# Feed-forward up slots in pairs by seven block products in place of eight, with weight block sums and gate times up on GpSimd

## The chip, the cores and the metric

The kernel runs on one core of one Trainium2 chip. The metric is device time in microseconds (us) of one execution. All data are f32. Every product is made in three fp32r passes: weights and activations are split into a high and a low part, and high x high, high x low and low x high are added in PSUM.

## What is computed

A two-layer block and then a second block, over 512 tokens of width 1024. Only the first block's feed-forward parts (two in each layer, four in all) are touched:

```python
def swiglu(x, w_gu, w_down):
    g, u = jnp.split(x @ w_gu, 2, axis=-1)
    return (jax.nn.silu(g) * u) @ w_down
...
h = h + 0.5 * swiglu(rmsnorm(h, ffn1_norm[i]), ffn1_w_gu[i], ffn1_w_down[i])
...
h = h + 0.5 * swiglu(rmsnorm(h, ffn2_norm[i]), ffn2_w_gu[i], ffn2_w_down[i])
```

The inner width is 2816, which is 22 tiles of 128 rows; each tile has a gate half and an up half. Between the two feed-forward parts of a layer stand a convolution branch and an attention branch, after them a gated projection; the second block follows the two layers. None of that is changed.

## The kernel before

**Slots.** The program is a list of slots. A slot is one weight tile of up to 8 x 128 rows by 128 columns: SyncE loads it into one of four places of `raw` (`load`), ScalarE copies it as fp32r into `w_hi` (`split_hi`, L673), VectorE writes `raw - w_hi` into `w_lo` (`split_lo`, L1688), and TensorE multiplies it with the 512 tokens in one of the four PSUM banks of `proj` (`slot_mm`, L1194 to L1196: for each of 8 k tiles three matmuls of 512 columns, 24 in all). Each engine has its own program in order; counters (`slot_done`, `slot_read`, `w_hi_ready`, `w_lo_ready`) hold them together. VectorE and ScalarE split a slot two slots before TensorE takes it (`AHEAD`).

**A feed-forward part** (`ffn` on each engine) has three groups of 8, 8 and 6 tiles (`FF_GROUPS`). A group is an up stage (two slots a tile, gate then up) and a down stage (8 slots that add to `h`). Behind each pair of up slots VectorE scales both results by `rs`, the inverse norm (L1704, from PSUM), ScalarE takes the tanh (L720), VectorE makes (tanh + 1) x gate (L1769) and times up (L1773), ScalarE rounds that to `a_hi` (L724), and VectorE takes the rest as `a_lo` (L1776). GpSimd does nothing in the up stages. It works in the last down stage of each part, where it squares and adds the columns of the new `h` for the next norm (`squares`, L563 to L568).

**The start of a part.** TensorE begins with slot 0 as soon as the normalized input `u_hi`, `u_lo` arrives, then makes the norm sum (L1215); ScalarE takes a root, VectorE the reciprocal `rs` (L1698), and only then are the results of the first slots read. The four banks hold them until then.

Of the kernel before, what the change touches and what calls it, by code (L numbers as in the profile page):

```python
# [147 lines left out]
def build(nc, I, out_t):  # L148
    ctx = ExitStack()
    with ctx:  # L150
# [25 lines left out]
        w_lo, _ = place("w_lo", RING * KD * P, F32R)  # L176
# [101 lines left out]
        pos_ready, sin_ready, c_tanh, lam_exp = (sem(n) for n in ("pos_ready", "sin_ready", "c_tanh", "lam_exp"))  # L278
# [20 lines left out]
        out_done = sem("out_done")  # L299

# [20 lines left out]


# [83 lines left out]
        HALF = S // 2  # L406
# [17 lines left out]
        def _(sp):  # L424
# [53 lines left out]
            for layer in range(DEPTH):  # L478
# [54 lines left out]
        def _(pool):  # L533
# [2071 lines left out]
```

## Time and profile before

| | us |
|---|---|
| median of 3 runs | 3029.08 (3026.34 to 3031.82) |
| the profiled execution, its own time | 3027.1 |
| its span in the trace | 3025.4 |
| VectorE busy | 1691.3 (56%) |
| ScalarE busy | 1104.4 (37%) |
| GpSimd busy | 303.9 (10%) |

The span runs from the first to the last instruction in the trace. A busy share is an average over stages, and says little of a single one. The prediction reads a stage from its own rows. A matmul's recorded duration has its way through the array in it, so that its pace is read from the distance between the starts of two matmuls, not from the duration.

### The profile page before, as it was taken

The page shows a single profiled execution, that of the slowest core. Times are in us where ns is not written, and L with a number is a line of the kernel's source. Part 1 is how long each engine was busy: PE and PEld are TensorE (multiplying, and loading weights), DVE is VectorE, ACT ScalarE, POOL GpSimd, SP SyncE. Part 2 cuts the span into 40 slices and gives each one's busy share as a digit, 9 for nine tenths or more (in the row PEclk, how much of TensorE's full clock was granted, in tenths as well). Part 3 has the DMA queues.
Part 4 walks back from the last instruction along what each step waited for, and adds up shares of the span by engine and source line. Part 5 has one row for each costly group of instructions (what it writes and reads, how often), then busy time and mean ns, then how long its engine had stood idle before and what let it go on. Part 6 is the DMA issues. An engine that isn't in the chain of part 4 may idle for free.

```text
span 3025.4 us, 36951 instructions
## 1 busy us (share of the span) xinstructions
PE 2989.9 (99%) x13582; PEld 2432.9 (80%) x13582; DVE 1691.3 (56%) x2381; ACT 1104.4 (37%) x1717; POOL 303.9 (10%) x248
## 2 busy tenths in 40 slices
PE   8999999999999999999999999999999999999999
PEld 7888888778888887888888888888888775688887
DVE  6655564565655557555456455555556767463334
ACT  4232333562332234322232454232323555552223
POOL 2000300000100012000030000200003215600000
PEclk9999999999999999999999999999999998999999
DMA  5332232123323223432232212333222420122232
GB/s 199 109 125 95 94 98 78 58 60 115 139 97 139 97 87 95 152 139 97 92 97 96 84 38 78 111 139 141 96 97 84 170 70 29 43 79 96 95 94 82
DMA packets 86804, 301.55 MB, mean 100 GB/s; under 512 B 10272, under 2 KB 19616, under 8 KB 85536
## 3 DMA queue, kind: packets, MB, share of 16 engines
q1 hardware_dynamic: 86688, 300.02, 30.0%
q8 instruction: 71, 1.16, 0.2%
q14 instruction: 45, 0.37, 0.0%
HBM read 297.88 MB, written 2.10 MB: 99 GB/s over the span
## 4 chain that ended last, share of the span: by engine, by line
PE 93%; DVE 3%; ACT 2%; POOL 1%; issue 1%; DMA 0%; DVEq 0%; SPq 0%; ACTq 0%
PE proj L1194 27%; PE proj L1196 27%; PE proj L1195 27%; PE ot L1341 1%; PE proj L1575 1%; PE proj L1577 1%; PE proj L1576 1%; DVE w_lo L1688 1%; PE sc L1575 1%; PE sc L1577 1%; PE sc L1576 1%; POOL work L644 1%; PE ot L1468 0%; PE tr L1301 0%; PE sc L1290 0%
## 5 line engine op out<-in xcount | busy, mean ns | idle before, releaser
L1194 PE MATMUL proj<-u_hi,w_hi 128*128 128x512 f32 x2632 | 1029.5, 391 | 13.6 <-DVE u_lo L1693 9.0
L1196 PE MATMUL proj<-u_hi,w_lo 128*128 128x512 f32 x2632 | 1021.6, 388 | 0.0
L1195 PE MATMUL proj<-u_lo,w_hi 128*128 128x512 f32 x2632 | 1021.6, 388 | 0.0
L1688 DVE TENSOR_TENSOR w_lo<-raw,w_hi 128x1024 fp32r<-128x1024 f32 (+4 forms) x567 | 657.2, 1162 | 492.1 <-ACT w_hi L673 482.9
L673 ACT ACTIVATE w_hi<-raw 128x1024 fp32r<-128x1024 f32 (+4 forms) x567 | 535.9, 954 | 334.9 <-PE proj L1196 212.9
L1194 PEld LDWEIGHTS proj<-u_hi,w_hi 128*128 128x128 f32 x2632 | 494.8, 188 | 122.8 <-issue 15.9
L1195 PEld LDWEIGHTS proj<-u_lo,w_hi 128*128 128x128 f32 x2632 | 495.0, 188 | 104.1 <-issue 3.1
L1196 PEld LDWEIGHTS proj<-u_hi,w_lo 128*128 128x128 f32 x2632 | 494.7, 188 | 101.9
L1194 PE MATMUL proj<-a_hi,w_hi 128*128 128x512 f32 x936 | 368.1, 393 | 3.4 <-DVE w_lo L1688 1.5
L1196 PE MATMUL proj<-a_hi,w_lo 128*128 128x512 f32 x936 | 364.9, 390 | 0.0
L1195 PE MATMUL proj<-a_lo,w_hi 128*128 128x512 f32 x936 | 364.5, 389 | 0.0
L1704 DVE TENSOR_TENSOR work<-proj,rs 128x512 f32<-128x512 f32 x260 | 179.3, 690 | 279.7 <-PE proj L1196 279.2
L724 ACT ACTIVATE a_hi<-work 128x512 f32 (+1 forms) x88 | 55.6, 632 | 437.3 <-DVE work L1773 437.3
L1194 PEld LDWEIGHTS proj<-a_hi,w_hi 128*128 128x128 f32 x936 | 175.8, 188 | 42.2 <-DVE a_lo L1776 3.0
L1196 PEld LDWEIGHTS proj<-a_hi,w_lo 128*128 128x128 f32 x936 | 175.7, 188 | 37.1
L1195 PEld LDWEIGHTS proj<-a_lo,w_hi 128*128 128x128 f32 x936 | 175.9, 188 | 34.7
L563 POOL TENSOR_TENSOR acc<-h 128x512 f32<-128x512 f32 x6 | 6.2, 1040 | 1500.7 <-DVE h L1791 1301.6
L1791 DVE SCALAR_TENSOR_TENSOR h<-proj,h 128x512 f32<-128x512 f32 x96 | 66.3, 691 | 159.6 <-PE proj L1196 159.5
L720 ACT ACTIVATE work<-work 128x512 f32<-128x512 f32 x88 | 55.6, 632 | 261.3 <-DVE work L1704 261.3
L1776 DVE TENSOR_TENSOR a_lo<-work,a_hi 128x512 f32 (+1 forms) x88 | 61.0, 693 | 78.9 <-ACT a_hi L724 78.9
L679 ACT ACTIVATE u_hi<-h,vec 128x512 fp32r<-128x512 f32 x48 | 34.8, 725 | 141.0 <-DVE h L1791 82.1
L566 POOL TENSOR_TENSOR sq<-h 128x512 f32<-128x512 f32 x42 | 62.1, 1479 | 72.4 <-DVE h L2041 40.0
(469 smaller groups left out, 2879.7 us busy)
## 6 DMA issues: line engine op xcount, KB each, us to landing
raw<-in_ffn_gu SPq DMA_DIRECT2D x174, 512.0 KB, 3.4
raw<-in_in_w SPq DMA_DIRECT2D x68, 512.0 KB, 3.3
raw<-in_ffn_dn SPq DMA_DIRECT2D x64, 512.0 KB, 3.3
raw<-in_ff SPq DMA_DIRECT2D x64, 512.0 KB, 3.4
gate<-in_ada SPq DMA_DIRECT2D x8, 3072.0 KB, 12.0
raw<-in_ffn_dn SPq DMA_DIRECT2D x32, 384.0 KB, 3.0
raw<-in_in SPq DMA_DIRECT2D x18, 512.0 KB, 3.4
raw<-in_mla_out SPq DMA_DIRECT2D x16, 512.0 KB, 3.4
```

Of the source, the lines that this page charges most:

```text
L566: pool.tensor_tensor(sq, x(m), x(m), ALU.mult).then_inc(sq_ready, 1)
L673: act.activation(wt(w_hi, slot, slot.tiles), wt(raw, slot, slot.tiles), ACT.Copy)\
L1194: pe.matmul(out, w_h, x_h, start=first, stop=False)
L1195: pe.matmul(out, w_h, x_l, start=False, stop=False)
L1196: return pe.matmul(out, w_l, x_h, start=False, stop=last)
L1575: pe.matmul(row_bank(half, t), span(hi(k), t), w_h, start=first and j + i == 0, stop=False, skip_group_check=True)
L1576: pe.matmul(row_bank(half, t), span(lo(k), t), w_h, start=False, stop=False, skip_group_check=True)
L1577: mm = pe.matmul(row_bank(half, t), span(hi(k), t), w_l, start=False, stop=last and j + i == 2, skip_group_check=True)
L1688: dve.tensor_tensor(wt(w_lo, slot, slot.tiles), wt(raw, slot, slot.tiles), wt(w_hi, slot, slot.tiles).bitcast(F32), ALU.subtract).then_inc ...
L1704: return dve.tensor_tensor(dst, proj[:, slot.pos, :], rs, ALU.mult)
L1776: dve.tensor_tensor(a_lo_t[:, at], work(8 + q), a_hi_t[:, at].bitcast(F32), ALU.subtract)\
L1791: dve.scalar_tensor_tensor(at, proj[:, slot.pos, :], 0.25, at, ALU.mult, ALU.add)\
```

## The change

In 72 of the 88 pairs of up slots (the first round of four slots of each part, and in the very first part the whole first group, stay as they are) the product of a pair of weight tiles with the tokens is made from blocks. The 1024 input rows are cut into two halves, the two tiles (gate and up) are the two block columns, and the 512 tokens are cut into two halves of 256. A 2 x 2 block product needs eight block products; Strassen's scheme, in Winograd's form, needs seven with sums of blocks. A block product is here 4 k tiles x 3 passes = 12 matmuls of 256 columns.

- TensorE (`pair_products`): 7 x 12 = 84 matmuls of 256 columns for each pair, in place of 48 of 512. A pair uses four half banks; three of them are used twice. Even pairs use `proj`, odd pairs `tr`, `ot` and `sc`.
- GpSimd (`pair_sums`): four weight block sums of 512 columns for each pair, written to `w_sum`, which lies on `w_lo`. It also adds the parts of the results (two adds of 256 columns, `part_sum`) and multiplies gate and up (`gate_times_up`, 512 columns).
- ScalarE: splits 3.5 x 1024 columns of weights for a pair (`pair_hi`) where it was 2 x 1024, and copies four parts of 256 columns from PSUM (`part_copy`); tanh and `a_hi` as before.
- VectorE: subtracts for 3.5 x 1024 columns (`pair_lo`), adds parts from PSUM (`first_half` 256 columns, `other_halves` 512), scales gate and up by `rs` in one instruction of 1024 columns in SBUF, then `pair_act` (tanh + 1 times gate x up) and `pair_a_lo` of 512 each.
- A weight place is now shared: a pair's block i lies where the pair before had its block i, and may be written once that product is done (`place_free`).
- At the start of each part, in the round of ordinary slots, sums of blocks of the input are made (`x_diffs`, 4 blocks): on VectorE five instructions of 1024 columns and later four of 1024 or 2 x 512 for the low parts, on GpSimd six of 512 and two of 1024, on ScalarE four splits.
- The first two down slots of each group are interleaved over k up to the last k tile. SyncE's load of the gated projection's input (`p_t`) is issued after the second part's last weights rather than before them. Several counters of other stages share one counter.

Cut to its core, the diff is:

```diff
-w_lo, _ = place("w_lo", RING * KD * P, F32R)
+w_lo, w_lo_at = place("w_lo", RING * KD * P, F32R)
+w_sum, _ = place("w_sum", RING * KD * P, at=w_lo_at)
...
+def paired_rounds(no, g):
+    return 0 if g < start_group(no) else FF_GROUPS[g] // 2 - (g == start_group(no))
...
+def done(self, i):
+    return ((slot_done, self.up.done) if self.odd and i == 6 else
+            (product_done, 13 * self.round + 7 * self.odd + i + 1))
+def place_free(self, i):
+    if self.opening or (i == 6 and not self.odd):
+        return slot_done, self.start.number + 1 + i // 2
+    return (product_done, 13 * self.round + i + 1) if self.odd else (product_done, 13 * (self.round - 1) + 7 + i + 1)
+def place(self, t, i, n=1):
+    o = (2 * self.start.pos + i) % (2 * RING) * S
...
+def banks(self):
+    if self.odd:
+        return tr[:, 0:HALF], ot[:, 0:HALF], sc[:, 0:2, 0:HALF]
+    p = self.start.pos
+    p2 = (p + 2) % RING
+    return proj[:, p, 0:HALF], proj[:, p + 1, 0:HALF], proj[:, p2:p2 + 2, 0:HALF]
...
+def pair_sums(p, which):
+    a11, a12 = (wt(raw, p.gate, KD)[:, j * S:(j + 1) * S] for j in range(2))
+    a21, a22 = (wt(raw, p.up, KD)[:, j * S:(j + 1) * S] for j in range(2))
+    s1, s3, s2, s4 = (p.place(w_sum, i) for i in (2, 3, 4, 5))
+    if which == 0:
+        pool.wait_ge(raw_in[p.gate.pos], p.gate.loads)
+        pool.wait_ge(raw_in[p.up.pos], p.up.loads)
+        pool.wait_ge(*p.place_free(2))
+        pool.tensor_tensor(s1, a21, a22, ALU.add).then_inc(block_sum, 1)
+        pool.wait_ge(*p.place_free(3))
+        pool.tensor_tensor(s3, a11, a21, ALU.subtract).then_inc(block_sum, 1)
+        return
+    pool.wait_ge(*p.place_free(4))
+    pool.wait_ge(block_sum, 4 * p.number + 1)
+    pool.tensor_tensor(s2, s1, a11, ALU.subtract).then_inc(block_sum, 1)
+    pool.wait_ge(*p.place_free(5))
+    pool.wait_ge(block_sum, 4 * p.number + 3)
+    pool.tensor_tensor(s4, a12, s2, ALU.subtract).then_inc(block_sum, 1)
...
+spare = t4_raw[:, 0:S]
+for j in range(2):
+    k = slice(2 * j, 2 * j + 2)
+    to = t3_raw(j)
+    step(four(to), x_hi_lo(u_hi_t, 1, 1)[:, k].bitcast(F32), x_hi_lo(u_hi_t, 0, 1)[:, k].bitcast(F32), ALU.subtract)
+    step(four(spare), x_hi_lo(u_lo_t, 1, 1)[:, k].bitcast(F32), x_hi_lo(u_lo_t, 0, 1)[:, k].bitcast(F32), ALU.subtract)
+    step(to, to, spare, ALU.add)
+pool.wait_ge(x_diff, XD * no + 5)
+step(four(t4_raw), x_hi_lo(u_hi_t, 1, 0).bitcast(F32), four(d_at(xd_f, 3)), ALU.subtract)
+step(four(t4_raw), four(t4_raw), x_hi_lo(u_lo_t, 1, 0).bitcast(F32), ALU.add)
...
+def gate_times_up(p):
+    pool.wait_ge(pair_scaled, p.number + 1)
+    pool.tensor_tensor(p.both[:, S:2 * S], p.both[:, 0:S], p.both[:, S:2 * S], ALU.mult).then_inc(sil_ready, 1)
+def ffn(layer, f):
+    no = 2 * layer + f
+    for g in range(start_group(no), len(FF_GROUPS)):
+        pairs = pairs_of(layer, f, g)
+        if g == start_group(no):
+            x_diffs(layer, f)
+        pair_sums(pairs[0], 0)
+        pair_sums(pairs[0], 1)
+        for n, p in enumerate(pairs):
+            after = pairs[n + 1:n + 2]
+            if n:
+                gate_times_up(pairs[n - 1])
+            for q in after:
+                pair_sums(q, 0)
+            pool.wait_ge(part_copied, p.copied + 3)
+            pool.tensor_tensor(part_b, part_b, part_c, ALU.add).then_inc(part_sum, 1)
+            for q in after:
+                pair_sums(q, 1)
+            pool.wait_ge(part_copied, p.copied + 4)
+            pool.wait_ge(part_sum, 2 * p.number + 1)
+            pool.tensor_tensor(p.both[:, 3 * HALF:4 * HALF], part_b, part_d, ALU.add).then_inc(part_sum, 1)
+        gate_times_up(pairs[-1])
...
+def part_copy(p, i):
+    product, bank, to = ((0, p.banks()[0], part_a), (2, p.banks()[2][:, 0], part_b),
+                         (3, p.banks()[2][:, 1], part_c), (4, p.banks()[0], part_d))[i]
+    act.wait_ge(*p.done(product))
+    if i == 0:
+        act.wait_ge(slot_read, p.start.number + RING + 2 * p.odd)
+    if i == 1 and p.number:
+        act.wait_ge(part_sum, 2 * p.number)
+    act.activation(to, bank, ACT.Copy).then_inc(part_copied, 1)
...
+for n, p in enumerate(pairs):
+    after = pairs[n + 1] if n + 1 < len(pairs) else None
+    pair_hi(p, 3)
+    part_copy(p, 0)
+    if n:
+        pair_tanh(pairs[n - 1])
+    if after:
+        pair_hi(after, 0)
+    else:
+        split_hi(down[0])
+    part_copy(p, 1)
+    part_copy(p, 2)
+    if n:
+        pair_a_hi(pairs[n - 1])
+    elif a_hi_before:
+        a_hi_before()
+        act.wait_ge(x_diff_pool, XP * no + 8)
+        act.wait_ge(slot_done, p.start.number + RING)
+        act.activation(x_hi_lo(u_hi_t, 0, 1), four(t4_raw), ACT.Copy).then_inc(x_diff_hi, 1)
+    part_copy(p, 3)
+    if after:
+        pair_hi(after, 1)
+        pair_hi(after, 2)
+    else:
+        split_hi(down[1])
...
+for i, (bank, n_half, opens) in enumerate(((b0, 0, True), (b1, 0, True), (b2, 0, True), (b3, 0, True),
+                                           (b0, 0, False), (b2, 1, False), (b3, 1, False))):
+    if i in (0, 1, 5, 6):
+        k_half = (0, 1, 0, 0, 0, 1, 0)[i]
+        x_h, x_l = (part(t, k_half, n_half) for t in (u_hi_t, u_lo_t))
+    else:
+        x_h, x_l = diff((0, 0, 0, 2, 1)[i])
+    if i == 2:
+        pe.wait_ge(block_lo, 2 * p.number + 2)
+        pe.wait_ge(x_diff, XD * p.no + 8)
+        if not p.odd:
+            pe.wait_ge(slot_read, p.start.number + RING)
+    if i == 4:
+        pe.wait_ge(w_lo_ready, p.gate.done)
+        pe.wait_ge(part_copied, p.copied + 1)
+    if i == 5:
+        pe.wait_ge(part_copied, p.copied + 2)
+    if i == 6:
+        pe.wait_ge(w_lo_ready, p.up.done)
+        pe.wait_ge(part_copied, p.copied + 3)
+        pe.wait_ge(x_diff, XD * p.no + 9)
+    for k in range(KD // 2):
+        w_h, w_l = p.weight(i, k)
+        mm = pe.matmul(bank, w_h, x_h(k), start=opens and k == 0, stop=False, skip_group_check=True)
+        if p.odd and k == 0 and i in (2, 4, 6):
+            mm.then_inc(slot_done, 1)
+        pe.matmul(bank, w_h, x_l(k), start=False, stop=False, skip_group_check=True)
+        mm = pe.matmul(bank, w_l, x_h(k), start=False, stop=k == KD // 2 - 1, skip_group_check=True)
+    mm.then_inc(slot_done if p.odd and i == 6 else product_done, 1)
...
+def first_half(p):
+    dve.wait_ge(*p.done(1))
+    dve.wait_ge(part_copied, p.copied + 1)
+    dve.tensor_tensor(p.both[:, 0:HALF], p.banks()[1], part_a, ALU.add).then_inc(slot_read, 1)
+def other_halves(p):
+    b23 = p.banks()[2]
+    dve.wait_ge(*p.done(6))
+    dve.wait_ge(part_copied, p.copied + 4)
+    dve.tensor_tensor(four(p.both[:, HALF:3 * HALF]), b23, part_d.unsqueeze(1).to_broadcast([P, 2, HALF]), ALU.add)\
+       .then_inc(slot_read, 1)
+    dve.wait_ge(*p.scaled())
+    dve.wait_ge(part_sum, 2 * p.number + 2)
+    both = p.both.rearrange("p (n s) -> p n s", n=2)
+    dve.tensor_tensor(both, both, rs.unsqueeze(1).to_broadcast([P, 2, S]), ALU.mult).then_inc(pair_scaled, 1)
+def pair_act(p):
+    dve.wait_ge(tanh_ready, p.count)
+    dve.wait_ge(sil_ready, p.count)
+    up = p.both[:, S:2 * S]
+    dve.scalar_tensor_tensor(up, work(4 + p.odd), 1.0, up, ALU.add, ALU.mult).then_inc(act_ready, 1)
...
+for n, p in enumerate(pairs):
+    after = pairs[n + 1] if n + 1 < len(pairs) else None
+    if n:
+        other_halves(pairs[n - 1])
+    pair_lo(p, 2)
+    pair_lo(p, 3)
+    if n == 0 and before:
+        before[0]()
+    first_half(p)
+    if after:
+        pair_lo(after, 0)
+    else:
+        split_lo(down[0])
+    if n:
+        pair_act(pairs[n - 1])
+        pair_a_lo(pairs[n - 1])
+    elif before:
+        before[1]()
+        dve.wait_ge(x_diff_hi, XH * no + 4)
+        dve.tensor_tensor(x_hi_lo(u_lo_t, 0, 1), four(t4_raw), x_hi_lo(u_hi_t, 0, 1).bitcast(F32), ALU.subtract)\
+           .then_inc(x_diff, 1)
+    if after:
+        pair_lo(after, 1)
+    else:
+        split_lo(down[1])
+other_halves(pairs[-1])
+pair_act(pairs[-1])
+pair_a_lo(pairs[-1])
```

## Rows read from the trace of the kernel before

**Rows 1.** The page: busy time by engine, and the chain that ended last.
```profile
PE 2989.9 (99%) x13582; PEld 2432.9 (80%) x13582; DVE 1691.3 (56%) x2381; ACT 1104.4 (37%) x1717; POOL 303.9 (10%) x248
PE 93%; DVE 3%; ACT 2%; POOL 1%; issue 1%; DMA 0%; DVEq 0%; SPq 0%; ACTq 0%
```
**Rows 2.** Waits of TensorE: waiting line, releaser, total us, times, longest.
```profile
PE proj L1194 <- DVE u_lo L1693: 9.0, 2, 8.4
PE proj L1194 <- DVE w_lo L1688: 3.1, 5, 0.8
```
**Rows 3.** Timeline of TensorE, 512 columns: start us, us; 30 matmuls lie between them.
```profile
2373.78 0.39 PE L1194 MATMUL proj<-u_hi,w_hi 128*128 128x512 f32 x1
...
2380.58 0.39 PE L1194 MATMUL proj<-u_hi,w_hi 128*128 128x512 f32 x1
```
**Rows 4.** Timeline of TensorE, 256 columns, second block: 30 matmuls from first to last.
```profile
2678.53 0.28 PE L1194 MATMUL proj<-u_hi,w_hi 128*128 128x256 f32 x1
...
2682.12 0.28 PE L1194 MATMUL proj<-u_hi,w_hi 128*128 128x256 f32 x1
```
**Rows 5.** Groups by form, stretch 810 to 850 us: count, busy us, mean ns, idle before.
```profile
L1688 DVE TENSOR_TENSOR w_lo<-raw,w_hi 128x1024 fp32r<-128x1024 f32 x8 | 9.8, 1226 | 10.0 <-ACT w_hi L673 9.7
L673 ACT ACTIVATE w_hi<-raw 128x1024 fp32r<-128x1024 f32 x7 | 7.3, 1046 | 0.0
L1704 DVE TENSOR_TENSOR work<-proj,rs 128x512 f32<-128x512 f32 x8 | 5.5, 690 | 5.8 <-PE proj L1196 5.8
L1773 DVE TENSOR_TENSOR work<-work 128x512 f32<-128x512 f32 x4 | 2.8, 692 | 0.4
L720 ACT ACTIVATE work<-work 128x512 f32<-128x512 f32 x4 | 2.5, 633 | 8.5 <-DVE work L1704 8.5
```
**Rows 6.** Groups by form, GpSimd, whole span.
```profile
L588 POOL TENSOR_TENSOR work<-work 128x512 f32<-128x512 f32 x6 | 7.8, 1293 | 44.0 <-ACT work L822 44.0
L578 POOL TENSOR_TENSOR acc<-acc,work 128x512 f32<-128x512 f32 x6 | 11.1, 1856 | 0.9
L644 POOL TENSOR_SCALAR work<-work,row_stats 128x512 f32<-128x512 f32 x16 | 24.9, 1571 | 13.6 <-DVE row_stats L2136 13.6
L644 POOL TENSOR_SCALAR work<-work,row_stats 128x256 f32<-128x256 f32 x8 | 7.3, 920 | 3.9 <-DVE row_stats L2136 3.9
```
**Rows 7.** Timeline of GpSimd and VectorE near 750 us: GpSimd began first.
```profile
750.59 1.28 POOL L568 TENSOR_TENSOR acc<-acc,sq 128x512 f32<-128x512 f32 x1
750.70 2.26 DVE L1688 TENSOR_TENSOR w_lo<-raw,w_hi 128x1024 fp32r<-128x1024 f32 x1 [1.08 <-ACT w_hi L673]
```
**Rows 8.** Timeline of both engines near 350 us: VectorE began first.
```profile
349.87 0.96 DVE L1688 TENSOR_TENSOR w_lo<-raw,w_hi 128x768 fp32r<-128x768 f32 x1 [0.87 <-ACT w_hi L673]
349.98 2.00 POOL L568 TENSOR_TENSOR acc<-acc,sq 128x512 f32<-128x512 f32 x1
```
**Rows 9.** Timeline of both engines near 2374 us: they take turns.
```profile
2373.49 1.29 POOL L613 TENSOR_TENSOR acc<-acc,work 128x512 f32<-128x512 f32 x1 [3.49 <-ACT work L900]
2374.17 1.16 DVE L2058 SCALAR_TENSOR_TENSOR h<-work,h 128x512 f32<-128x512 f32 x1
2374.74 1.74 POOL L614 TENSOR_TENSOR sq<-sq,ax 128x512 f32<-128x512 f32 x1
2375.26 1.51 DVE L1688 TENSOR_TENSOR w_lo<-raw,w_hi 128x256 fp32r<-128x256 f32 x1
```
**Rows 10.** Timeline near 587 us: VectorE reads PSUM and one SBUF tile.
```profile
586.28 1.29 POOL L594 TENSOR_TENSOR ux<-ux,sq 128x512 f32<-128x512 f32 x1 [40.19 <-ACT ux L766]
586.93 0.69 DVE L1921 TENSOR_TENSOR u_lo<-ot,u_hi 128x512 fp32r<-128x512 f32 x1
```
**Rows 11.** Timeline, VectorE at the start of the second feed-forward part.
```profile
787.93 3.35 DVE L1698 RECIPROCAL rs<-acc 128x512 f32<-128x512 f32 x1 [4.22 <-ACT acc L683]
791.20 1.16 DVE L1688 TENSOR_TENSOR w_lo<-raw,w_hi 128x1024 fp32r<-128x1024 f32 x1
```
**Rows 12.** Windows: from:to, us, busy us (x instructions) by engine, PEclk, DMA share, GB/s.
```profile
2388.00:2392.00 4.00, 2.00 (x5) 0.57 (x3) 2.18 (x4) 3.45 (x6) 0.00 (x0) 1.00 0.85 360
2510.00:2515.00 5.00, 2.20 (x15) 1.54 (x13) 4.69 (x11) 0.42 (x1) 0.19 (x1) 0.99 0.27 105
2515.00:2520.00 5.00, 4.73 (x42) 2.80 (x44) 1.76 (x6) 1.52 (x4) 0.00 (x0) 0.50 0.02 5
```

More of the change, by code:

```diff
@@ new lines, in pairs_of @@
+        def pairs_of(layer, f, g):
+            return [Pair(layer, f, g, at) for at in range(2 * paired_rounds(2 * layer + f, g))]
+        HALF = S // 2
+        XD, XP, XH = 9, 8, 4
+        x_at = work_at + 8 * S * 4
+        xd_r, _ = place("x_split", 10 * S, F32R, at=x_at)
+        xd_f, _ = place("x_diffs", 10 * S, at=x_at)
+        four = lambda x: x.rearrange("p (k s) -> p k s", s=HALF)
+        x_hi_lo = lambda x_t, k_half, n_half: x_t.rearrange("p (m s) -> p m s", s=S)[
+            :, KD // 2 * k_half:KD // 2 * (k_half + 1), HALF * n_half:HALF * (n_half + 1)]
@@ L323, in build @@
+        d_at = lambda t, i: t[:, 2 * i * S:2 * (i + 1) * S]
+        t3_lo = lambda j: (a_hi_t, a_lo_t)[j][:, 8 * S:9 * S]
+        t3_raw = lambda j: (ax(8), ax(17))[j]
+        t4_raw = ax_t[:, 6 * S:8 * S]
+        part_a, part_b, part_c, part_d = (work_t[:, 6 * S + j * HALF:6 * S + (j + 1) * HALF] for j in range(4))
         L2 = DEPTH
@@ new lines, in pair_tanh, with pair_a_hi, paired @@
+            def pair_tanh(p):
+                act.wait_ge(pair_scaled, p.number + 1)
+                act.activation(work(4 + p.odd), p.both[:, 0:S], ACT.Tanh, scale=0.5).then_inc(tanh_ready, 1)
+            def pair_a_hi(p):
+                act.wait_ge(act_ready, p.count)
+                act.activation(a_hi(p.tile), p.both[:, S:2 * S], ACT.Copy).then_inc(a_hi_ready, 1)
+            def paired(layer, f, g, a_hi_before):
+                no = 2 * layer + f
+                down = [Slot(layer, STAGE[f"ffn{f + 1}_down{g}"] + j) for j in range(AHEAD)]
+                pairs = pairs_of(layer, f, g)
+                for n, p in enumerate(pairs):
[23 more added lines that the diff above has]
+                        split_hi(down[1])
+                pair_tanh(pairs[-1])
+                pair_a_hi(pairs[-1])
@@ L1775, in up @@
-                            at = bass.ds((2 * it + q) * S, S)
-                            dve.tensor_tensor(a_lo_t[:, at], work(8 + q), a_hi_t[:, at].bitcast(F32), ALU.subtract)\
-                               .then_inc(a_lo_ready, 1)
-                    repeat(dve, s0, ft // 2, RING, up, first or passed)
+                            if starts:
+                                (x_diffs_lo if q else x_diffs)(no)
+                            if starts and q:
+                                pair_lo(Pair(layer, f, g, 0), 1)
+                            elif 2 * q + 1 + AHEAD >= opened:
+                                split_lo(Slot(layer, s0 + 2 * q + 1 + AHEAD, it, RING))
```

325 lines of the change are left out of this document (252 added, 73 removed).

## The prediction

> **What bounds the kernel now.** I read the page first. TensorE is busy for 99% of the span, and 93% of the chain that ended last is TensorE [rows 1]. Its longest waits sum to 12 us, and 8.4 of them are one wait at the very start [rows 2]. So the kernel ends when TensorE has issued its matmuls, and in the stages that are changed nothing else is late: in 40 us of an up stage VectorE waits 15.8 us ahead of its splits and scalings [rows 5]. The timeline then gives the pace. Between the two starts of [rows 3] lie 30 matmuls of 512 columns: 6.80 / 30 = 0.2267 us each. A pair of up slots is 48 of them, 10.88 us. This is the time against which each part below stands.
>
> **What TensorE saves.** Matmuls of 256 columns with their own weights stand in the second block: 3.59 / 30 = 0.1197 us each [rows 4]. The 84 of a pair take 10.05 us, so a pair saves 0.83 us and 72 pairs 59 us. The weight loads do not bind at that pace.
> The Trainium skill, "TensorE: Matmul & The Clock Gate", section "Back-to-back issue gap", gives 131 ns for 512 columns and 81 ns for 128 in a sustained stream, which would be about 98 ns for 256 (an estimate between its two figures). By it a pair would go from 6.3 to 8.2 us and the change would lose 1.9 us a pair. The trace does not agree (227 and 120 ns), and I go by the trace.
>
> **What the helpers must do in a pair.** Taken one by one, each engine fits under 10.05 us. VectorE: `pair_lo` 3 x 1.226 + 0.69, the scaling 1.226, `pair_act` and `pair_a_lo` 2 x 0.692, and from PSUM 0.69 and about 0.4: 8.1 us [rows 5]. ScalarE: 3 x 1.046 + 0.6 for weights, four copies of 256 columns at about 0.4, two of 0.633: 6.6 us [rows 5]. GpSimd: five instructions of 512 columns at 1.293 and two of 256: I take 0.75 for one of these, between half of 1.293 and 0.92, the row of a one-input instruction of that width; 8.0 us in all [rows 6].
>
> **But VectorE and GpSimd do not run side by side.** In [rows 7] GpSimd's add ends at 751.87. VectorE's split, begun 0.11 us after it, takes 2.26 us where 1.226 is usual [rows 5] and ends 1.09 us after GpSimd's end. In [rows 8] it is the other way round: VectorE ends at 350.83, and GpSimd's add takes 2.00 in place of 1.293 and ends 1.15 us after that. In [rows 9] they take turns four times: ends at 2374.78, 2375.33, 2376.48 and 2376.77, so 0.55 us for VectorE with 512 columns, 1.15 for GpSimd, 0.29 for VectorE with 256. Whole instructions exclude each other where VectorE reads two SBUF operands. Where it reads PSUM and one SBUF operand they don't: 0.69 us in the middle of a GpSimd add, as without it [rows 10].
> [...] Were the contention partial, the sum below would shrink towards the fast rival's; the trace shows a full block.
>
> So I add the claims of both engines on this one resource, at 1.09 / 0.55 us for 1024 / 512 columns on VectorE and 1.15 on GpSimd:
> - VectorE: `pair_lo` 0, 1, 2 and the scaling, 4 x 1.09; `pair_lo` 3, `pair_act`, `pair_a_lo`, 3 x 0.55: 6.0 us.
> - GpSimd: four block sums and gate times up, 5 x 1.15; two adds of 256 columns, 0.58 to 0.78 each, taken as 0.6: 6.95 us.
> Together 13.0 us. I followed the two orders in the diff once round. Counted from the end of a pair's scaling: `pair_lo` 2 to 1.1, gate times up 2.3, `pair_lo` 3 2.8, sum 1 4.0, `pair_lo` 0 5.1, sum 3 6.3, `pair_act` 6.8, part add 7.4, sum 2 8.6, `pair_a_lo` 9.1, sum 4 10.3, `pair_lo` 1 11.4, part add 12.0, next scaling 13.2. Each is ready when its turn comes, so the period is 13.2 us. TensorE's products 4, 5, 6, 0 and 1 follow `pair_lo` 2 and end at 8.4; it then waits 3 us for `pair_lo` 1 before product 2. ScalarE has half of its time free. Bounds: 12.6 (the 256-column adds at their least and less for each turn) to 14.2 (1 us a period in which the resource lies idle between a semaphore and the next start).
>
> **The waits that are added.** TensorE's product 2 waits for `pair_lo` 1, and with it all later products; `pair_lo` 1 stands behind `pair_a_lo` and that behind ScalarE's `a_hi`. VectorE's scaling waits for GpSimd's last add, which stands behind block sums 2 and 4 of the next pair; behind the scaling stand the next pair's `pair_lo` 2 and 3, for which products 4 and 6 wait. This ring runs through both engines.
>
> **The sum.**
> 1. Interior pairs. The groups have 6 pairs (eight of them) or 8 (three). First and last pair have less to do: no pair before, no pair after. So 8 x 4 + 3 x 6 = 50 periods of 13.2 in place of 10.88: +116 us (86 to 166).
> 2. Ends of 11 groups. From the first product to the first scaling's end I count 13.4 us, and from the last interior scaling to TensorE's last product 5.5: 18.9 in place of 21.8, so -2.9 each, -32 us. What follows in the down stage is covered: the last `a_lo` is ready 7 us after the last product, and the first two down slots have 42 matmuls (9.5 us) that do not need it.
> 3. Starts of 4 parts. In the four ordinary slots the resource must carry `x_diffs` on VectorE (5 x 1.14 one behind the other), on GpSimd 6 x 1.15 + 2 x 2.3, the low parts 3.4, four block sums 4.6, and the usual splits and products, 6.4: some 32 us. `rs` comes at 791.3, five us after slot 0 is done [rows 11]; behind it VectorE has a split, the first scaling and then the five `x_diffs` before the split of slot 3. That split ends near 803.6 and TensorE wants it at 798.8: 4.8 us. `pair_lo` 0 is late by 4.6, `pair_lo` 1 by 4.0, slot 2 by 0.8, and the first pair's backlog is 4 us longer than in other groups: 18 us, in three of the parts. The first part starts it in its second group, where `rs` is long there: 15. Together +69 us (35 to 100).
> 4. Nothing: the moved load of `p_t` (issued at the start of the last down stage, some 35 us before it is read, and the queue in front of it has then only weights already asked for), the counters shared by stages, ScalarE's work, weight traffic (1 MB a pair in 10 us or more, where windows show up to 360 GB/s [rows 12]), and more program code to fetch. If code does not come in time, some us each group; covered by the range.
>
> 116 - 32 + 69 = +153 us. On the profiled execution's 3027.1 that is 3180; the median of the runs stands 2 us higher, so 3182.
>
> **The rivals.**
> - *TensorE stays the bound (faster).* If the claims of both engines overlap after all, or fall between each other's waits, each engine alone is under 10.05 us and the pairs run at TensorE's pace: -59, and about 3 us at each start: 3027 - 59 + 12 = 2980. The point from which it decides is a joint claim under 10.05 us. For it: busy sums of 8 us. Against it: three stretches with full exclusion [rows 7 to 9]. Chance 0.09.
> - *Slower still by the clock.* TensorE would wait 3 us in each period. After 2.28 us and 0.8 us of waiting in a window with little work its granted clock went to 0.50, the lower level, 1.2 GHz, in the next window; after a wait of 2.0 in 4 us it stayed at 1.00 [rows 12]. If it falls in most periods, the matmuls behind a wait take twice as long for about 5 us. Part of that goes into the wait itself; I take 1.5 us of a period and 6 us of a start: 50 x 1.5 + 4 x 6 = +99, 3281. Chance 0.17.
> - *Same.* If block sums slip into times in which VectorE works from PSUM or waits, and starts cost 8 us, gains and losses could cancel: a period of 11.2: 50 x 0.3 - 32 + 32, about 3042, with zero inside its spread. Chance 0.03.
> The rest, 0.71, is the forecast. What this kernel's measurement can tell from no change is 0.2%, 6 us. Faster 0.09, same 0.03, slower 0.88. The range reaches from the low ends of steps 1 and 3 (3027 + 86 - 32 + 35 = 3116, a little less for a period under 12.6) into the clock case: 3095 to 3275.
>
> **What the profile would show.** GpSimd and VectorE each busy most of the up stages, their instructions stretched: block sums of 512 columns at a mean of 1.7 to 2.3 us, `pair_lo` of 1024 columns near 1.9 to 2.2. Scaling instructions 13.2 us apart within a group. TensorE waiting for `pair_lo` before product 2, some 3 us a pair, its busy share near 93%, and 15 to 20 us lost at each start. Matmuls of 256 columns 0.12 us apart between waits. Wrong if the scalings stand 10.1 us apart and the block sums take 1.3 us: then two SBUF operands do not exclude GpSimd here, and the time is near 2980. The clock case shows as PEclk under 1.0 in the up stages and matmuls 0.24 us apart.

## The result, and the profile of the changed kernel

| | before | after |
|---|---|---|
| median of the runs, us | 3028.97 (3026.34 to 3031.82, 4 runs) | 3198.56 (3197.45 to 3200.09, 4 runs) |
| profiled execution, us | 3027.1 | 3200.1 |
| its span, us | 3025.4 | 3198.4 |

The changed kernel takes 1.056 times as long (95% interval 1.0542 to 1.0578). The forecast was 3182, within 3095 to 3275.

The page after: busy time by engine, and the chain that ended last; they answer to [rows 1].
```profile
PE 3008.8 (94%) x16174; PEld 2566.7 (80%) x16174; DVE 2187.2 (68%) x2565; ACT 1313.5 (41%) x2160; POOL 1189.0 (37%) x784
PE 68%; DVE 17%; POOL 7%; issue 5%; ACT 2%; DMA 0%; SPq 0%; DVEq 0%; POOLq 0%; ACTq 0%
```
TensorE was 93% of the chain and is 68% of it now; VectorE and GpSimd have 24% between them. GpSimd looks idle for 63% of the span. That is an average over stages, and says nothing of the up stages.

The waits of TensorE after (waiting line, releaser, total us, times, longest), against some 12 us in all in [rows 2]:
```profile
PE proj L1544 <- DVE work L2113: 69.7, 24, 3.3
PE sc L1544 <- DVE w_lo L2068: 32.8, 23, 2.7
PE proj L1544 <- DVE w_lo L2068: 20.0, 4, 11.5
PE proj L1448 <- DVE w_lo L2005: 13.8, 10, 3.6
PE proj L1544 <- DVE work L2021: 10.5, 4, 4.2
PE proj L1544 <- DVE u_lo L2154: 9.9, 4, 3.7
```
L1544 is the first matmul of each three in a pair's product, L2068 a 1024-column `pair_lo`, L2113 the addition of `other_halves` that empties the pair's PSUM banks. The first two rows are 47 waits in the middle of groups. The other four belong to the starts of the parts, but for seven waits of under 0.8 us in the fourth row.

Groups by form of the whole span after (count, busy us, mean ns, idle before); they answer to [rows 5, 6]:
```profile
L2068 DVE TENSOR_TENSOR w_lo<-w_sum,w_hi 128x1024 fp32r<-128x1024 f32 x72 | 142.5, 1980 | 40.8 <-POOL w_sum L680 40.8
L2118 DVE TENSOR_TENSOR work<-work,rs 128x1024 f32<-128x1024 f32 x72 | 88.2, 1225 | 18.6 <-POOL work L734 13.5
L676 POOL TENSOR_TENSOR w_sum<-raw 128x512 f32<-128x512 f32 x72 | 151.0, 2098 | 1.9 <-PE proj L1548 1.9
L712 POOL TENSOR_TENSOR work<-work 128x512 f32<-128x512 f32 x72 | 148.7, 2065 | 120.4 <-DVE work L2118 120.4
L683 POOL TENSOR_TENSOR w_sum<-raw,w_sum 128x512 f32<-128x512 f32 x72 | 127.3, 1768 | 10.6 <-POOL w_sum L680 0.4
L674 POOL TENSOR_TENSOR w_sum<-raw 128x512 f32<-128x512 f32 x72 | 122.2, 1697 | 261.8 <-PE proj L1450 191.3 <-PE proj L1548 68.8 <-PE sc L1548 1.7
```
Alone, 1024 columns take VectorE 1.226 us and 512 take GpSimd 1.293. Of these groups only the scaling (L2118) keeps its time, 1.225: GpSimd waits for it (120.4 us over 72 pairs), so nothing runs beside it.

One period. VectorE's timeline after (start us, us, line, operands):
```profile
905.55 1.22 DVE L2118 TENSOR_TENSOR work<-work,rs 128x1024 f32<-128x1024 f32 x1
906.70 1.22 DVE L2071 TENSOR_TENSOR w_lo<-w_sum,w_hi 128x1024 fp32r<-128x1024 f32 x1
907.83 1.77 DVE L2071 TENSOR_TENSOR w_lo<-raw,w_hi 128x512 fp32r<-128x512 f32 x1
909.53 0.41 DVE L2106 TENSOR_TENSOR work<-proj,work 128x256 f32<-128x256 f32 x1
909.86 1.97 DVE L2068 TENSOR_TENSOR w_lo<-raw,w_hi 128x1024 fp32r<-128x1024 f32 x1
911.75 1.78 DVE L2124 SCALAR_TENSOR_TENSOR work<-work 128x512 f32<-128x512 f32 x1
914.23 1.71 DVE L2128 TENSOR_TENSOR a_lo<-work,a_hi 128x512 fp32r<-128x512 f32 x1 [0.70 <-ACT a_hi L892]
915.86 2.31 DVE L2068 TENSOR_TENSOR w_lo<-w_sum,w_hi 128x1024 fp32r<-128x1024 f32 x1
918.09 0.68 DVE L2113 TENSOR_TENSOR work<-proj,work 128x512 f32<-128x512 f32 x1
918.87 1.23 DVE L2118 TENSOR_TENSOR work<-work,rs 128x1024 f32<-128x1024 f32 x1
```
GpSimd's in the same time:
```profile
906.86 2.20 POOL L712 TENSOR_TENSOR work<-work 128x512 f32<-128x512 f32 x1 [1.41 <-DVE work L2118]
909.01 1.73 POOL L674 TENSOR_TENSOR w_sum<-raw 128x512 f32<-128x512 f32 x1
911.09 1.90 POOL L676 TENSOR_TENSOR w_sum<-raw 128x512 f32<-128x512 f32 x1 [0.34 <-PE proj L1548]
912.95 1.19 POOL L729 TENSOR_TENSOR work<-work 128x256 f32<-128x256 f32 x1
914.09 1.30 POOL L680 TENSOR_TENSOR w_sum<-w_sum,raw 128x512 f32<-128x512 f32 x1
915.54 1.55 POOL L683 TENSOR_TENSOR w_sum<-raw,w_sum 128x512 f32<-128x512 f32 x1
917.05 1.72 POOL L734 TENSOR_TENSOR work<-work 128x256 f32<-128x256 f32 x1
```
The scalings stand 13.32 us apart. Read the ends: GpSimd 909.06, VectorE 909.60, GpSimd 910.74, VectorE 911.83, GpSimd 912.99, VectorE 913.53. The steps are 0.54, 1.14, 1.09, 1.16, 0.54: one engine at a time, at the claims of the forecast (a claim is the time for which an instruction keeps the other engine out). `other_halves` (L2113), which reads PSUM, takes its usual 0.68 beside GpSimd.

Three windows of the trace after, each from one scaling to the next (us; busy us by engine, PE, PEld, DVE, ACT, POOL; PEclk; DMA share; GB/s):
```profile
878.96:892.26 13.30, 10.09 (x82) 9.69 (x81) 12.50 (x9) 6.64 (x13) 11.74 (x7) 1.00 0.26 79
892.26:905.55 13.29, 9.97 (x82) 9.57 (x81) 12.50 (x9) 5.93 (x10) 11.74 (x7) 0.95 0.22 79
905.55:918.87 13.32, 13.32 (x89) 13.16 (x90) 12.52 (x9) 6.16 (x11) 11.43 (x7) 0.79 0.27 79
```
Both helpers are busy for some 12 of 13.3 us. TensorE waits 3.2 us of the first two; in the third its mean clock is 0.79 (a mix of the two levels, 1.2 and 2.4 GHz) and it fills the 13.3 us with the same work. The period is the same at either clock.

By TensorE's own stretches, from the start of a group's first product to that of its last matmul and one pace more (us; * with the part's four ordinary slots ahead):

| group | before | after | change |
|---|---|---|---|
| part 1, groups 1*, 2 | 87.04, 65.28 | 110.90, 73.22 | +31.8 |
| part 2, groups 0*, 1, 2 | 88.01, 87.04, 65.28 | 113.10, 99.80, 73.18 | +45.8 |
| part 3 | 89.52, 87.04, 65.28 | 116.80, 99.83, 74.41 | +49.2 |
| part 4 | 88.01, 87.04, 65.28 | 111.95, 99.84, 73.26 | +44.7 |

The sum, +171.5, is nearly all of the 173.0 between the two profiled executions. A group of 8 pairs is 6 x 13.31 + 19.96, one of 6 is 4 x 13.31 + 19.96; 49 of the 50 periods in the middle of groups are 13.29 to 13.35 us, and one is 14.36.

### The profile page after: what moved, and what is told of

Same layout as the page of the kernel before. It is cut to its first block, busy times and chain, and to the rows that moved or that the text cites. A ratio compares the mean times of both kernels' runs of the same rounds, so it can differ in the third digit from the quotient of the medians.

```text
span 3198.4 us, 43438 instructions
## 1 busy us (share of the span) xinstructions
PE 3008.8 (94%) x16174; PEld 2566.7 (80%) x16174; DVE 2187.2 (68%) x2565; ACT 1313.5 (41%) x2160; POOL 1189.0 (37%) x784
## 4 chain that ended last, share of the span: by engine, by line
PE 68%; DVE 17%; POOL 7%; issue 5%; ACT 2%; DMA 0%; SPq 0%; DVEq 0%; POOLq 0%; ACTq 0%
PE proj L1448 17%; PE proj L1450 16%; PE proj L1449 16%; DVE w_lo L2068 4%; DVE w_lo L2071 2%; POOL w_sum L683 2%; DVE work L2124 2%; POOL work L734 1%; POOL w_sum L680 1%; DVE a_lo L2128 1%; DVE work L2118 1%; POOL w_sum L674 1%; PE ot L1658 1%; PE proj L1892 1%; PE proj L1893 1%
## 5 line engine op out<-in xcount | busy, mean ns | idle before, releaser
L2005 DVE TENSOR_TENSOR w_lo<-raw,w_hi 128x1024 fp32r<-128x1024 f32 (+3 forms) x423 | 487.5, 1157 | 339.4 <-ACT w_hi L832 337.6
L1448 PE MATMUL proj<-u_hi,w_hi 128*128 128x512 f32 (+1 forms) x1480 | 583.3, 394 | 24.1 <-DVE w_lo L2005 12.3
L1450 PE MATMUL proj<-u_hi,w_lo 128*128 128x512 f32 (+1 forms) x1480 | 575.1, 389 | 0.0
L1449 PE MATMUL proj<-u_lo,w_hi 128*128 128x512 f32 (+1 forms) x1480 | 574.9, 388 | 0.0
L832 ACT ACTIVATE w_hi<-raw 128x1024 fp32r<-128x1024 f32 (+3 forms) x423 | 382.8, 918 | 215.4 <-PE proj L1450 93.7
L1448 PEld LDWEIGHTS proj<-u_hi,w_hi 128*128 128x128 f32 x1480 | 279.4, 189 | 90.8 <-DVE w_lo L2005 16.1
L1449 PEld LDWEIGHTS proj<-u_lo,w_hi 128*128 128x128 f32 x1480 | 279.5, 189 | 58.8 <-issue 3.1
L1450 PEld LDWEIGHTS proj<-u_hi,w_lo 128*128 128x128 f32 x1480 | 279.1, 189 | 57.5
L1544 PE MATMUL proj<-x_split,w_hi 128*128 128x256 f32 x432 | 140.2, 325 | 80.7 <-DVE work L2113 69.7
L1544 PE MATMUL proj<-u_hi,w_hi 128*128 128x256 f32 x576 | 167.8, 291 | 29.9 <-DVE w_lo L2068 20.0
L712 POOL TENSOR_TENSOR work<-work 128x512 f32<-128x512 f32 x72 | 148.7, 2065 | 120.4 <-DVE work L2118 120.4
L2068 DVE TENSOR_TENSOR w_lo<-w_sum,w_hi 128x1024 fp32r<-128x1024 f32 x72 | 142.5, 1980 | 40.8 <-POOL w_sum L680 40.8
L1544 PEld LDWEIGHTS proj<-x_split,w_hi 128*128 128x128 f32 x432 | 97.6, 226 | 86.8 <-DVE work L2113 74.6
L1547 PE MATMUL proj<-u_lo,w_hi 128*128 128x256 f32 x576 | 167.0, 290 | 0.0
```

Source lines behind the costliest of these rows:

```text
L712: pool.tensor_tensor(p.both[:, S:2 * S], p.both[:, 0:S], p.both[:, S:2 * S], ALU.mult).then_inc(sil_ready, 1)
L832: act.activation(wt(w_hi, slot, slot.tiles), wt(raw, slot, slot.tiles), ACT.Copy)\
L1448: pe.matmul(out, w_h, x_h, start=first, stop=False)
L1449: pe.matmul(out, w_h, x_l, start=False, stop=False)
L1450: return pe.matmul(out, w_l, x_h, start=False, stop=last)
L1544: mm = pe.matmul(bank, w_h, x_h(k), start=opens and k == 0, stop=False, skip_group_check=True)
```

## The experiments

All are edits of the changed kernel, each timed beside the kernel before (3028.94, 3027.29 and 3028.63 us in the three sets). "Ratio" is to that kernel.

**psum_lo: VectorE no longer reads two SBUF tiles in `pair_lo`.**
```diff
-  dve.tensor_tensor(lo, p.place(w_sum, at, n) if i else wt(raw, p.gate, KD), hi, ALU.subtract)
+  dve.tensor_tensor(four(lo), psum_part(p, i, n), four(hi), ALU.is_gt)
```


> This kernel takes the second SBUF operand away from VectorE's pair_lo: its first operand is a PSUM bank that TensorE does not use at that time (the low parts of the paired weights are thereby not the true ones; counts, widths, order and waits stay). Theory (whole instructions exclude each other where VectorE reads two SBUF operands): the joint claim in a pair falls from 13.1 to 2.2 + 6.95 = 9.1 us, under TensorE's 10.05, so the scalings stand 10.1 us apart and the time is about 3030 us (3005 to 3060), block sums take 1.3 to 1.6 us. Rival (the ring of waits between VectorE, GpSimd and ScalarE sets the period, not the exclusion): no operation is shorter, so the period stays at 13.3 us and the time at 3199. Rival (granted clock): between the two, with the period near 12.


Measured 3033.25 us, ratio 1.0013 (1.0003 to 1.0022). VectorE's and GpSimd's instructions near 867 us, and the window of a whole group of eight pairs (same columns as above):
```profile
867.26 1.22 DVE L2075 TENSOR_TENSOR w_lo<-sc,w_hi 128x1024 fp32r<-128x1024 f32 x1
867.92 1.30 POOL L676 TENSOR_TENSOR w_sum<-raw 128x512 f32<-128x512 f32 x1
```
```profile
925.62:1006.42 80.80, 80.80 (x674) 80.80 (x673) 66.40 (x70) 46.03 (x77) 60.79 (x51) 1.00 0.42 149
```
`pair_lo` and the block sum lie over each other and neither is longer for it; TensorE never waits in this group. The scalings in the middle of groups stand 10.03 to 10.11 us apart, but for the first two of each group (10.5 to 10.9). Waits and queues are the same as in the changed kernel; new are the PSUM operand, a comparison in place of the subtraction, and one fill ahead of everything. A `pair_lo` of 1024 columns takes 1.21 to 1.23 us all the same. So the 13.3 us were the exclusion, and not a ring of waits. It is taken away from `pair_lo` alone: `pair_a_lo` still takes up to 1.71 us here, and the instructions of the starts read SBUF as before. The forecast's TensorE pace (10.05) holds too. But the time is only that of before: 72 x 0.8 = 58 us won in the pairs are lost at the four starts, 14.7 us each (part 2's first group takes 97.93 us, which is 9.9 over the 88.01 of before although its six pairs save 4.8).

**sums_memset: the block sums read nothing.**
```diff
-  pool.tensor_tensor(s1, a21, a22, ALU.add).then_inc(block_sum, 1)
+  pool.memset(s1, 0.125).then_inc(block_sum, 1)      # s3, s2, s4 alike
```


> GpSimd's four block sums of each pair become fills of the same 512 columns, which read nothing from SBUF (the sums are thereby not formed). In the run with one-input multiplications VectorE was no longer held off, but GpSimd's instructions were stretched to 1.6 to 2.6 us by VectorE's. If the exclusion is about GpSimd's reads, the claims are 6.0 + 1.15 + 1.2 = 8.4 us, the period is TensorE's 10.05 us, the fills take 0.53 us whatever VectorE does, and the time is about 3018 us (3000 to 3040). If fills are held off too, the period is 4 x 0.45 longer: 10.2, and the fills' mean is near 1 us. If the ring of waits sets the period: near 3199 less 4 x 0.75 a pair, 3050.


Measured 3023.37, ratio 0.9985 (0.9976 to 0.9995), scalings 10.08 apart. One row of its groups:
```profile
L676 POOL MEMSET w_sum<- 128x512 f32 x72 | 38.0, 528 | 51.3 <-PE proj L1548 30.8 <-PE sc L1548 20.5
```
A fill takes 0.52 to 0.53 us wherever it falls (288 of them), and does not hold VectorE off: `pair_lo` 0 and 1 are back at a mean of 1.23 us.

**one_input: the block sums read one tile.**
```diff
-  pool.tensor_tensor(s1, a21, a22, ALU.add).then_inc(block_sum, 1)
+  pool.tensor_scalar(s1, a21, ones[:, 0:1], None, ALU.mult).then_inc(block_sum, 1)      # s3, s2, s4 alike
```


> GpSimd's four block sums of each pair become one-input multiplications of the same width (the sums are thereby not formed). If only two-input instructions of GpSimd exclude VectorE, the claim falls by 4 x 1.15 to 8.5 us, the period is TensorE's 10.1 us and the time about 3020 us (2995 to 3060). If every instruction of GpSimd that reads SBUF excludes it, one-input ones of 512 columns took 1.57 us before, so the period is 13.3 to 14.5 and the time 3200 to 3255 us. If the ring of waits sets the period, 3200 to 3255 us as well.


Measured 3206.04, ratio 1.0586 (1.0567 to 1.0605), scalings 13.46 apart. GpSimd's timeline, then VectorE's:
```profile
984.23 2.00 POOL L674 TENSOR_SCALAR w_sum<-raw,ones 128x512 f32<-128x512 f32 x1
986.22 2.17 POOL L676 TENSOR_SCALAR w_sum<-raw,ones 128x512 f32<-128x512 f32 x1
988.36 0.74 POOL L729 TENSOR_TENSOR work<-work 128x256 f32<-128x256 f32 x1
989.08 1.56 POOL L680 TENSOR_SCALAR w_sum<-raw,ones 128x512 f32<-128x512 f32 x1
990.81 2.59 POOL L683 TENSOR_SCALAR w_sum<-raw,ones 128x512 f32<-128x512 f32 x1 [0.17 <-PE proj L1548]
```
```profile
985.06 1.37 DVE L2068 TENSOR_TENSOR w_lo<-raw,w_hi 128x1024 fp32r<-128x1024 f32 x1
986.36 0.68 DVE L2124 SCALAR_TENSOR_TENSOR work<-work 128x512 f32<-128x512 f32 x1
987.74 0.69 DVE L2128 TENSOR_TENSOR a_lo<-work,a_hi 128x512 fp32r<-128x512 f32 x1 [0.70 <-ACT a_hi L892]
990.75 1.23 DVE L2068 TENSOR_TENSOR w_lo<-w_sum,w_hi 128x1024 fp32r<-128x1024 f32 x1 [2.32 <-POOL w_sum L680]
```
The time fits one expectation and the trace the other. VectorE is hardly held off any more (0.68 and 1.23 us in the middle of GpSimd's instructions, at most 0.33 us more in any `pair_lo` 0 or 1, and some 4.7 us idle in a period). But GpSimd's one-input instruction takes 1.56 us alone and in these rows 2.00 to 2.59 beside VectorE, also where GpSimd began first (984.23 before 985.06). GpSimd is busy for 11.9 of the 13.46 us and waits for the scaling in nearly all the rest, so its own sequence now sets the period. The exclusion has become nearly one-sided.

**all_dve: GpSimd's part of the pairs on VectorE.** The block sums (but the first pair's), the two 256-column additions and gate times up stand in VectorE's queue, in the places in which their readers want them:
```diff
+  dve_sum(after, 0)      # behind pair_lo(after, 0); the others behind pair_act, part_bc, pair_lo(after, 1)
```


> In the paired stages everything of GpSimd goes to VectorE (block sums of all but a group's first pair, both part adds, gate times up); only the input's block sums and the first pair's sums stay on GpSimd. Theory: nothing excludes any more, VectorE's own work is 4 x 1.14 + 8 x 0.6 + 3 x 0.33 + 0.6 = about 11.0 us a pair with 0.2 to 0.4 of waits for itself, so the period is 11.2 to 11.4 us, groups are about as long as before the change and only the four starts cost, 14 us each: 3085 us (3065 to 3110). Rival (VectorE is already the bound because of its many instructions): moving 3.7 us more to it makes it slower than 3199. Rival (ring of waits): a shorter ring, any time between 3050 and 3199, with VectorE idle over 2 us in a period.


Measured 3107.0, ratio 1.0256 (1.0237 to 1.0274), scalings 11.65 apart. Two of the sixteen or so instructions of a period:
```profile
986.80 0.69 DVE L2102 TENSOR_TENSOR w_sum<-raw 128x512 f32<-128x512 f32 x1
987.58 0.69 DVE L2142 TENSOR_TENSOR a_lo<-work,a_hi 128x512 fp32r<-128x512 f32 x1
```
The first is a block sum: 0.69 us here, where it claimed 1.15 on GpSimd. With everything on one engine the kernel is 92 us faster than with two engines at work. It stays over 10.05 us a pair, since VectorE alone now has 11.65.

**gate_up_dve: gate times up back on VectorE alone.**
```diff
+  dve.wait_ge(pair_scaled, p.number + 1)
+  dve.tensor_tensor(up, p.both[:, 0:S], up, ALU.mult).then_inc(sil_ready, 1)
```


> Gate times up goes from GpSimd back to VectorE, everything else stays. Theory (exclusion): 1.15 us of claim are replaced by 0.55, so the period falls from 13.3 to 12.7 us and the time to about 3166 us (3155 to 3180). Rival (GpSimd's own order is the bound, without exclusion): the period falls by the whole 1.25 us of that instruction or more, time about 3130 us. Rival (VectorE's own work is the bound): the period rises by 0.6, about 3230 us.


Measured 3183.53, ratio 1.051 (1.0491 to 1.0529); periods of 12.67 to 13.16, 13.07 in the mean of the 50 in the middle of groups. The claims fall by 1.15 - 0.55 = 0.6, the mean period by 0.24. In its waits of TensorE one row grew:
```profile
PE proj L1541 <- DVE work L2110: 77.9, 25, 3.2
```
That is product 2 waiting for `other_halves` of the pair before, which empties the banks it writes. GpSimd in turn waits for TensorE's products. Either a ring through the banks sets the rest, or the claims are larger than I counted; the next two runs tell.

**early: the PSUM addition of `other_halves` ahead of `pair_lo` 1 of the next pair.**
```diff
                     if after:
+                        other_halves(p)          # the addition alone
                         pair_lo(after, 1)
```


> VectorE's other_halves addition, which reads PSUM, is put ahead of pair_lo 1 of the next pair, where it can run beside GpSimd's block sum 4, and TensorE's banks come free 1.8 us earlier. Theory (the sum of the claims is the period): nothing changes, 13.3 us and 3199 us (3190 to 3203), only TensorE waits for pair_lo 1 instead of the addition. Rival (the ring through TensorE's banks sets the period): 0.6 to 0.7 us less a period, 3165 us.


Measured 3201.72, ratio 1.0576 (1.0558 to 1.0594), scalings 13.31 apart as before the edit. TensorE's waits have only moved to another releaser (the first row has the four waits at the starts in it, 20.0 us in the changed kernel):
```profile
PE proj L1544 <- DVE w_lo L2068: 81.3, 29, 11.5
PE sc L1544 <- DVE w_lo L2068: 44.8, 25, 2.7
```
In the changed kernel the banks were thus never the bound, although the largest row of its waits named them.

**gate_up_early: both edits.**


> Gate times up on VectorE, and other_halves ahead of pair_lo 1. With the first alone the period was 13.13 us, not the 12.7 of the sum of claims; in the trace GpSimd stood idle for 3.7 us for TensorE's product 2, which waited 3.1 us for the addition that frees its banks. If this ring is what kept the 0.4 us, the period is now 12.7 us or less and the time 3160 us (3145 to 3170). If not, it stays at 3184.


Measured 3171.26, ratio 1.0478 (1.0461 to 1.0496). 38 of the 50 periods in the middle of groups are 12.49 to 12.72 us, most of the others 13.15; the mean is 12.69, against 13.31. With the ring opened, the 0.6 us of the claims come out in the mean. Why the shortest periods are 0.8 shorter and others only 0.15 was not looked into.

**diffs_late: at the starts, `x_diffs` behind the split of slot 3.**
```diff
                             normed(Slot(layer, s0 + 2 * q + 1, it, RING), ...)
-                            if starts:  (x_diffs_lo if q else x_diffs)(no)      # stood ahead of the split
```


> At the start of a part VectorE's five x_diffs instructions come after the split of slot 3, not before. TensorE's wait of 3.6 us for slot 3 goes. Theory (the start is bound by the sum of the claims of both engines): the same instructions are late for the next waits, pair_lo 0 and pair_lo 1, and 0 to 4 us are won over the four starts: 3197 us (3190 to 3202). Rival (each wait is a fault of order of its own): 4 x 3.6 and more are won, 3184 us or less.


Measured 3200.03, ratio 1.0571 (1.0554 to 1.0589). In the changed kernel TensorE waits at the start of part 2 twice; its timeline:
```profile
834.35 0.50 PE L1448 MATMUL proj<-u_hi,w_hi 128*128 128x512 f32 x1 [3.65 <-DVE w_lo L2005]
...
843.92 0.57 PE L1544 MATMUL proj<-u_hi,w_hi 128*128 128x256 f32 x1 [3.84 <-DVE w_lo L2068]
...
1311.06 0.58 PE L1544 MATMUL proj<-u_hi,w_hi 128*128 128x256 f32 x1 [11.51 <-DVE w_lo L2068]
```
The same place in diffs_late:
```profile
843.78 0.57 PE L1544 MATMUL proj<-u_hi,w_hi 128*128 128x256 f32 x1 [8.31 <-DVE w_lo L2068]
```
The first wait is gone, the second has taken it over, and the first pair begins at 843.78 us, where it was 843.92. Part 3 of the changed kernel (the row at 1311.06) shows this without an edit.

**diff_fills and psum_lo_diff_fills: the thirteen instructions of `x_diffs` read nothing,** in the changed kernel and in psum_lo.
```diff
-  pool.tensor_tensor(to, x, y, op).then_inc(x_diff_pool, 1)
+  pool.memset(to, 0.0).then_inc(x_diff_pool, 1)      # on dve alike, with x_diff
```


> The thirteen instructions of x_diffs (five on VectorE, eight on GpSimd, at each of the four starts) are fills that read nothing; their low and high parts are still split, so the products with the input's differences use other data. Each start now costs 17 us. Theory (a start is late by the sum of the claims on the resource that the two engines share): the x_diffs are 5 x 1.14 + 6 x 1.15 + 2 x 2.3 = 17 of some 32 us of claims against 22 us of ordinary slots; without them no slot of the start is late, and what stays is the first pair's own backlog, 3 to 5 us. Four starts less 12 to 14 us: 3150, range 3143 to 3158; TensorE's waits for slot 3 (3.6) and before the first pair's product 0 (3.8, once 11.5) gone. Rival (the starts are late by the order of the waits on VectorE, rs and the splits of the input's parts, not by claims): only the time of the five VectorE instructions behind rs goes, some 3.6 us a start: 3184.

> As diff_fills, and pair_lo reads a PSUM bank for its first operand as in psum_lo. psum_lo came out at 3033 because its pairs save 0.8 us each (58 us) and its four starts cost 14.7 us each (59 us). Theory: the starts' cost is the x_diffs; without them 2 to 4 us of it stay: 3033 - 4 x 12 = 2985, range 2975 to 2995, faster than the kernel before by some 44 us, which is what seven products for eight would give if the helpers were free. Rival (order of waits): 3033 - 14 = 3019.


Measured 3171.0, ratio 1.0473 (1.0456 to 1.0491), and 3005.65, ratio 0.9926 (0.991 to 0.9943): 28 us less each, 7 a start. Both theories missed (12 and 3.6 a start). VectorE at the start of part 2 in psum_lo_diff_fills shows why:
```profile
792.28 0.91 DVE L2095 MEMSET x_diffs<- 128x1024 f32 x1 [0.28 <-DVE x_diffs L2095]
793.47 0.91 DVE L2095 MEMSET x_diffs<- 128x1024 f32 x1 [0.28 <-DVE x_diffs L2095]
794.30 1.16 DVE L2005 TENSOR_TENSOR w_lo<-raw,w_hi 128x1024 fp32r<-128x1024 f32 x1
```
My expectation took VectorE's fills as nearly free. They are 1.19 us apart, the five cost 6 us of the queue ahead of slot 3's split, and TensorE still waits for that split (1.8), `pair_lo` 0 (1.1), the slot's product L2021 (2.6) and the input's last low part (0.9). So about half of a start's cost in psum_lo (7 of 14.7 us) goes with the reads of `x_diffs`. That is not the joint claims alone: the fills are also shorter in themselves, GpSimd's eight most of all (six of 512 columns take 3.44 us, where the additions took 1.28 to 2.16 each). The other half is what stands one behind the other in VectorE's own queue. How much of that half the fills themselves are was not measured.

## Why the prediction was right, step by step

- **TensorE's pace.** 0.1197 us for 256 columns: in psum_lo periods of 10.05 came out. Right.
- **Exclusion, and the sum of claims.** 13.0 us forecast by the sum, 13.31 measured, and the fourteen turns of the period above stand in the order that I wrote down. The 13.2 that I used has no cause: the order has no gap in it, and its steps are the same claims as the sum (12.96), rounded up one by one. That rounding put 12 us into step 1 in the right direction, by luck. What really comes on top is 0.36 us in the period above: the scaling, which waits for GpSimd's last add, ends 1.33 us after it and not 1.09; block sum 2, which follows an add of GpSimd itself, ends 1.26 us after it and not 1.15. The exclusion is shown from both sides: taking it away on VectorE's side (psum_lo) or on GpSimd's (sums_memset) gives 10.1; moving one claim gives its 0.6 once the banks are not late; one engine in place of two gives 11.65.
- **Step 1, interior pairs.** 50 x (13.31 - 10.88) = +121.5 us, forecast +116.
- **Step 2, ends of groups.** 11 x (19.96 - 21.76) = -19.8, forecast -32: the mis-sized term. I had 13.4 us from a group's first product to its first scaling's end. In the group that begins at 969.34 that scaling ended at 983.65, so 14.3: the first block sum could not start before 973.99, when a place for it came free, and the last one was stretched by `pair_lo` 1 to 2.33 us. The other side is 5.7 for 5.5.
- **Step 3, starts.** The rest of +171.5 is +69.8, forecast +69: 16 to 19 each. The size is right, in part by luck. The waits of part 2 are at slot 3 (3.65, forecast 4.8), `pair_lo` 0 (3.84, 4.6) and the slot's product before product 2 (1.82, 4.0), and one I had only as "backlog": product 6 of the first pair waits 3.7 us for the input's last low part. They sum to 13 of that start's 17.2 us; what the rest is was not measured (the clock, below, is one candidate). The account by claims alone was not borne out, as the last two runs show: my 32 us of claims stood for a lateness that is in part VectorE's own queue.
- **Step 4, nothing.** The table leaves 1.5 us for everything outside the up stages. The errors all have one sign: 5.5, 12.2, 0.8 and 1.5 us are the 20 us between 3180 and the 3200.1 of the profiled execution.
- **Where TensorE waits.** Before product 2, as written, but 2.9 us in the mean in even pairs and 1.4 in odd ones; and in even pairs the last to come was `other_halves` and not `pair_lo` 1. Both stand in one queue behind the same claims, so nothing hung on it (early).
- **The rivals.** *TensorE stays the bound*: its deciding point, a joint claim under 10.05, was not met. Where it was met (psum_lo) the starts cost 14.7 and not 3, so its 2980 was far too low as well. What the change would take with no exclusion at all is not shown: in psum_lo the starts still had it, and without the reads of `x_diffs` it was 3005.65. *The clock*: it did fall, as this rival says, in 19 of the 50 periods in the middle of groups, to means of 0.79 to 0.88, but at no cost: those periods are 13.30 to 13.35 us long, those at 0.99 or 1.00 are 13.29 to 13.34. The period is the claims', and a slower TensorE spends its waiting time on it. At the starts this is not shown. There too the clock fell, in part 2 also around the last of the start's waits (the window below), and the first period of that group is the one of 14.36 us: the clock may have cost about 1 us there, and no run separates it. The mean over the span is 0.973. *Same* was not near.

That window of the trace after (same columns as above):
```profile
859.85:866.67 6.82, 5.73 (x27) 5.76 (x28) 5.91 (x5) 1.92 (x3) 4.51 (x3) 0.50 0.02 4
```

The Trainium skill, "SBUF — State Buffer", section "Who interferes with whom", says that VectorE with two SBUF inputs contends with a GpSimd instruction that reads SBUF, not with one that only writes it, and that this contention is an exclusive lock. The trace agrees for GpSimd's two-input instructions (turns of 0.54, 1.14, 1.09 us) and for fills (0.53 us). It does not for one-input instructions, which read SBUF too: there VectorE's 512 columns kept their 0.68 us, and only GpSimd was held, 2.00 to 2.59 us for 1.56.

## What to carry to other kernels

Before work is moved to an idle engine, ask what the two share: here VectorE (two SBUF operands) and GpSimd (two operands) are one resource, and their claims add up, at GpSimd's price of 1.15 us against VectorE's 0.55 for the same 512 columns. Their sum against the pace of the bound, 13.0 against 10.05, gave the sign, and the period to 0.3 us. The starts of stages need an account of their own: a fill in place of each read won only 7 of 14.7 us there. And the releaser with the largest total of waits need not be the bound: the edit that removes it can leave the period as it was.

## What was not expected of the hardware

- A GpSimd instruction with one tile as input made no `pair_lo` 0 or 1 of VectorE longer by more than 0.33 us, but is itself stretched by it, from 1.56 to mostly 2.0 to 2.6 us at 512 columns (at most 3.10). A fill (0.53 us) neither holds off nor is stretched.
- VectorE's fill of 1024 fp32 columns takes 0.91 us, and the next one, which waits for it, starts 1.19 us after it did; with two-input instructions it is 1.26 (800.87 to 802.13 us in psum_lo).
- A period in which TensorE's clock was down (0.79) was as long as one at 1.00, and the windows show it as a busier TensorE (13.32 for 10.09 us): a higher busy share is no sign of less waiting.
